# Expert results added to token rows in DRAM by accumulating DMAs, in place of a gather behind the last tile

## What is computed

```python
xn = rms_norm(x, norm2_g)
# router: one of 4 groups, then the top 2 of its 4 experts; combine[token, expert] is the weight, zero elsewhere
y = 0
for e in range(16):
    h = silu(xn @ w_gate[e]) * (xn @ w_up[e])        # 1024 -> 512
    y = y + combine[:, e:e+1] * (h @ w_down[e])      # 512 -> 1024
x = x + y
out = rms_norm(x, final_norm_g)
```

## Time and profile before

| | us |
|---|---|
| median of 3 runs (791.05 to 791.95) | 791.48 |
| the profiled execution, its own time | 791.86 |
| its span in the profile | 789.3 |
| PE busy | 764.9 (97%) |
| DVE busy | 493.4 (63%) |
| ACT busy | 450.4 (57%) |
| POOL busy | 208.8 (26%) |

### The profile page before, as it was taken

How to read it: one execution, slowest core, us unless ns; L and a number is a source line. 1 busy time by engine, 2 the same in 40 slices (tenths; PEclk the granted TensorE clock), 3 DMA queues, 4 the chain that set the end, 5 groups by cost and what they waited for, 6 DMA issues and landing times.

```text
span 789.3 us, 10839 instructions
## 1 busy us (share of the span) xinstructions
PE 764.9 (97%) x3739; PEld 622.0 (79%) x3739; DVE 493.4 (63%) x702; ACT 450.4 (57%) x590; POOL 208.8 (26%) x124
## 2 busy tenths in 40 slices
PE   7999999999999999999999999999999999999994
PEld 4788777777787888888888788887778888888782
DVE  5704476576644302322022668999999999999888
ACT  5244656565553323323221546887888887888862
POOL 3644433232233444344442522000000000000033
PEclk9999999999999999999999999999999999999998
DMA  8569999782122253323327537999999999999965
GB/s 299 183 215 386 365 333 388 276 329 81 54 81 81 81 193 100 108 81 105 102 86 264 194 114 275 404 409 408 409 410 409 409 410 409 409 409 356 395 253 205
DMA packets 134318, 206.74 MB, mean 262 GB/s; under 512 B 10813, under 2 KB 65669, under 8 KB 134278
## 3 DMA queue, kind: packets, MB, share of 16 engines
q1 hardware_dynamic: 126084, 188.80, 65.7%
q10 hardware_dynamic: 5890, 9.04, 3.1%
q0 software_dynamic: 2304, 8.39, 2.9%
HBM read 157.95 MB, written 48.25 MB: 261 GB/s over the span
## 4 chain that ended last, share of the span: by engine, by line
PE 82%; DVE 7%; ACT 2%; ACTq 2%; issue 2%; DMA 2%; POOL 2%; DVEq 0%; SPq 0%; POOLq 0%
PE ps L1052 24%; PE ps L1054 24%; PE ps L1053 24%; DVE w_lo L389 3%; PE ps L1342 2%; PE ps L1146 1%; PE ps L1174 1%; PE ps L1157 1%; PE ps L1295 1%; POOL raw_mg L656 1%; PE ps L1269 1%; DMA x<-in_x 1%; PE ps L1349 1%; ACTq L877 1%; DVE xT_lo L1959 1%
## 5 line engine op out<-in xcount | busy, mean ns | idle before, releaser
L383 POOL TENSOR_TENSOR w_lo<-raw,w_hi 128x1024 fp32r<-128x1024 f32 x72 | 173.6, 2414 | 253.1 <-ACT w_hi L371 253.1
L371 ACT ACTIVATE w_hi<-raw 128x1024 fp32r<-128x1024 f32 x73 | 76.9, 1058 | 191.9 <-PE ps L1054 164.4
L1052 PE MATMUL ps<-xn_hi,w_hi 128*128 128x512 f32 x352 | 140.6, 399 | 0.0
L1054 PE MATMUL ps<-xn_hi,w_lo 128*128 128x512 f32 x352 | 137.2, 390 | 0.0
L1053 PE MATMUL ps<-xn_lo,w_hi 128*128 128x512 f32 x352 | 137.1, 389 | 0.0
L1052 PE MATMUL ps<-w_hi,xT_hi 128*128 128x512 f32 (+1 forms) x248 | 97.0, 391 | 2.2 <-DVE w_lo L389 2.2
L1054 PE MATMUL ps<-w_hi,xT_lo 128*128 128x512 f32 (+1 forms) x248 | 95.2, 384 | 0.0
L1053 PE MATMUL ps<-w_lo,xT_hi 128*128 128x512 f32 (+1 forms) x248 | 94.9, 383 | 0.0
L656 POOL DMA_INDIRECT raw_mg<-slots,slot_idx x7 | 7.8, 1117 | 280.4 <-DMA slots<-y_tile 278.6
L1052 PEld LDWEIGHTS ps<-xn_hi,w_hi 128*128 128x128 f32 x352 | 66.1, 188 | 16.2 <-issue 2.0
L1053 PEld LDWEIGHTS ps<-xn_lo,w_hi 128*128 128x128 f32 x352 | 66.1, 188 | 14.0 <-issue 1.0
(11 more groups left out here) (311 smaller groups left out, 1476.3 us busy)
## 6 DMA issues: line engine op xcount, KB each, us to landing
slots<-raw SPq DMA_DIRECT2D x65, 512.0 KB, 7.2
raw<-in_w_in SPq DMA_DIRECT2D x52, 512.0 KB, 4.1
raw_mg<-in_exp_w_down SPq DMA_DIRECT2D x35, 512.0 KB, 11.0
raw<-in_exp_w_gate SPq DMA_DIRECT2D x29, 512.0 KB, 11.6
raw_a<-in_exp_w_gate SPq DMA_DIRECT2D x26, 512.0 KB, 11.0
raw_c<-in_exp_w_up SPq DMA_DIRECT2D x24, 512.0 KB, 11.9
raw_mg<-in_exp_w_up SPq DMA_DIRECT2D x22, 512.0 KB, 11.1
raw<-in_exp_w_up SPq DMA_DIRECT2D x15, 512.0 KB, 11.7
```

Source lines behind the costliest of these rows:

```text
L371: nc.scalar.activation(w_hi[:, b % HI_SLOTS, :], raw_buf(b), ACT.Copy)\
L383: eng.tensor_tensor(w_lo[:, b % HI_SLOTS, :], raw_buf(b), w_hi[:, b % HI_SLOTS, :].bitcast(F32), ALU.subtract)\
L1052: pe.matmul(dst, hi_l, hi_r, start=start, stop=False)
L1054: return pe.matmul(dst, lo_l, hi_r, start=False, stop=stop)
```

## The change

**Weights with the slots.** A DRAM tensor `info` holds, for each slot, the token's number and its weight (8 bytes). POOL fills it with "no token" (numbers from 512 up, weight 0) during the mixer, scatters the 1024 real entries with 8 indirect DMAs behind `weighed`, reads the whole back into `slot_info` (64 KB) and raises `info_in`. For this the weights are worked out before tile 1 and no longer between tiles 4 to 6. ACT waits for `info_in` ahead of the first block that it splits inside `tile(at_odd(0), 0)`.

**Adding in DRAM.** SP stores `x_rows` (the residual) to a DRAM tensor `acc` in two halves of 1 MB. Behind each tile ACT's copy out of PSUM multiplies by the row's weight (same instruction, with `scale`), into one buffer `y_home`, and POOL adds the 128 rows to their tokens' rows in `acc` by one indirect DMA with `compute_op=add`, one after the other. ACT no longer stores.

**The end.** When the tile before the last has been added, SP loads all of `acc` into `x_rows`, and these rows are normed and written out. POOL gathers from `acc` the rows of the last tile's own 128 tokens (`z_home`); the last tile's result is added to them by DVE, they are normed apart, and written by an indirect DMA over the rows just written. The selection matrix, its matmuls and the gathers from `slots` go.

The core of the diff:

```diff
@@ SP
+            sp.dma_start(acc[TOK:TOK + P, :], raw[:, 4, :]).then_inc(S["zeros_stored"], 16)
+            def store_x2(half):
+                at = slice(512 * half, 512 * (half + 1))
+                sp.wait_ge(S["x2_done"], NT * (half + 1))
+                sp.dma_start(acc[0:TOK, at].rearrange("(t p) n -> p t n", p=P), x_rows[:, :, at])\
+                  .then_inc(S["acc_in"], 16)
             for r in range(8):
                 if r == RAW_MIX + 1:
+                    store_x2(0)
                     sp.wait_ge(S["w_used"], B_EXP)
                 load_block(ODD, r, tile_source(1, 0, r))
+            store_x2(1)
...
+            sp.wait_ge(S["y_added"], n_stop * 16 + 16 * (PAIRED - 1))
+            for t in range(NT):
+                sp.dma_start(x_rows[:, t, :], acc[t * P:(t + 1) * P, :]).then_inc(rows_in[t], 16)
@@ POOL
+            pool.wait_ge(S["info_filled"], 16)
+            pool.wait_ge(S["weighed"], 2)
             for t in range(NT):
-                gather(0, y_lo(t), t)
-                gather(1, y_hi(t), t)
+                for k in range(2):
+                    pool.indirect_dma_start(
+                        info, bass.IndirectOffsetOnAxis(ap=info_idx[:, 0, 2 * t + k:2 * t + k + 1], axis=0),
+                        pick_info[:, t, k, :], None).then_inc(S["info_out"], 16)
+            pool.wait_ge(S["info_out"], 16 * 2 * NT)
+            pool.dma_start(info_words, info.rearrange("(p b) n -> p (b n)", p=P)).then_inc(S["info_in"], 16)
+            def add_result(j, block):
+                if j is not first:
+                    pool.wait_ge(S["y_added"], j * 16)
+                pool.tensor_copy(tokens[:, :], info_words[:, bass.ds(block * 2, 1)]).then_inc(S["tokens_in"], 1)
+                pool.wait_ge(S["acc_in"], 32)
+                pool.wait_ge(S["tokens_in"], j + 1)
+                pool.wait_ge(S["y_act"], j + 1)
+                pool.indirect_dma_start(acc, bass.IndirectOffsetOnAxis(ap=tokens[:, 0:1], axis=0), y_home, None,
+                                        compute_op=ALU.add).then_inc(S["y_added"], 16)
...
+            pool.wait_ge(rows_in[0], 32)
+            link(pool.tensor_tensor(y_weighed, x_rows[:, 0, :], gf_rows[:, :], ALU.mult))
+            y_power(0)
+            pool.wait_ge(S["y_rstd"], 1)
+            pool.tensor_scalar(y_weighed, y_weighed, stat[:, 7, 0:1], None, ALU.mult).then_inc(S["y_norm_pool"], 1)
+            for t in range(1, NT):
+                y_power(t)
+            pool.wait_ge(S["z_stat"], 1)
+            pool.tensor_tensor(stat[:, 4, 3:4], stat[:, 4, 2:3], minus_half[:, :], ALU.pow).then_inc(S["z_rstd"], 1)
+            pool.wait_ge(S["z_norm"], 2)
+            pool.wait_ge(S["y_out"], 16 * NT)
+            pool.indirect_dma_start(out[0], bass.IndirectOffsetOnAxis(ap=last_info[:, 0:1], axis=0), z_weighed, None,
+                                    bounds_check=TOK - 1, oob_is_err=False).then_inc(S["z_out"], 16)
@@ ACT, y_part
-                act.wait_ge(at.y_free, at.y_count)
-                act.activation(at.y, ps[:, 5:7, :].rearrange("p a n -> p (a n)"), ACT.Copy).then_inc(S["y_act"], 1)
-                act.wait_ge(S["y_act"], n + 1)
-                act.dma_start(slots[bass.ds(block * P, P), :], at.y).then_inc(at.y_free, 16)
+                act.wait_ge(S["tokens_in"], n)
+                act.activation(y_home, ps[:, 5:7, :].rearrange("p a n -> p (a n)"), ACT.Copy,
+                               scale=info_words[:, bass.ds(block * 2 + 1, 1)].bitcast(F32)).then_inc(S["y_act"], 1)
             split_hi_loop(at_odd(0), AHEAD)
+            act.wait_ge(S["info_in"], 16)
             tile(at_odd(0), 0)
...
-            hT_hi_half(1)
-            for c in range(2):
-                act.wait_ge(S["w_used"], loop_block(tiles, 3 + c))
-                act.activation(xT_hi[:, 4 * c:4 * c + 4, :].rearrange("p k n -> p (k n)"), ps[:, 5 + c, :], ACT.Copy)\
-                   .then_inc(S["xT_hi_done"], 1)
+            y_square(0)
+            hT_hi_half(1)
+            for t in range(1, NT):
+                y_square(t)
@@ DVE
             overflow_count()
-            overflow_tiles(0, block_table, NE * PER_EXPERT)
+            info_rows()
+            share_of(0)
+            share_of(1)
+            combine_weights()
             for r in range(AHEAD):
                 split_lo_loop(at_odd(0), r)
...
+            y_normed(1)
+            y_normed(2)
+            dve.wait_ge(S["z_in"], 16)
+            z_sum(0)
+            z_weigh(0)
+            y_normed(3)
+            z_sum(1)
+            z_weigh(1)
```

More of the change, by code:

```diff
@@ L294, in build @@
             "x_even_in x_odd_in xT_ps xT_hi_done xT_done silu_done hid_done hT_ps hT_hi_done hT_done "
-            "y_act y_even_stored y_odd_stored y_last_stored before_last_stored sel_ps sel_done z_ps "
-            "y_sum y_sq y_stat y_rstd y_norm y_out dve_chain").split()}
+            "acc_in info_filled weighed info_out info_in tokens_in y_act y_added z_in "
+            "y_sq y_rstd y_norm_pool y_norm_dve z_sum z_weighed z_sq z_stat z_rstd z_norm y_out z_out pool_chain dve_chain").split()}
         raw_in = [sem(f"raw_in{s}") for s in range(RAW_MIX)]
@@ new lines, in block_of @@
+            def block_of(i):
+                return pool.value_load(block_table[0:1, bass.ds(i + 1, 1)], min_val=0, max_val=SLOT_TILES - 1)
+            first = 0
+            add_result(first, 0)
+            add_result(1, PER_EXPERT)
+            pool.wait_ge(S["tab"], 1)
+            n_stop = pool.value_load(tile_table[0:1, 0:1], min_val=NE - PAIRED, max_val=MAX_TILES - PAIRED)
+            with pool.Fori(2, n_stop + (PAIRED - 1)) as j:
+                add_result(j, block_of(j))
+            last_block = block_of(n_stop + (PAIRED - 1))
@@ L1850, in full_tables @@
                 dve.tensor_copy(tile_table[:, 1:NE + 1], row(23, NE)).then_inc(S["tab"], 1)
-            def last_tile():
-                for n in range(2):
-                    dve.tensor_scalar(last_rows[:, n:n + 1], four(2)[:, 0:1], 0.0,
-                                      float((NE - 1) * PER_EXPERT), ALU.is_equal, ALU.mult)
-                link(dve.tensor_tensor(weight, over, row(25, NE, PER_EXPERT - 1), ALU.mult))
-                link(dve.tensor_reduce(last_rows[:, 2:3], weight.rearrange(flat), AX.X, ALU.max))
@@ L1859, in last_tile_rows @@
-            def last_tile_rows():
-                for n in range(2):
-                    link(dve.tensor_tensor(last_rows[:, n:n + 1], last_rows[:, n:n + 1], last_rows[:, 2:3], ALU.max))
-                    dve.tensor_scalar(last_rows[:, n:n + 1], last_rows[:, n:n + 1], float(P), float(n * P),
-                                      ALU.mult, ALU.add)
-            at_first, at_second = top_slot[:, :, 1], top_slot[:, :, 0]
-            swap, apart = four(6), four(7)
-            in_last, place_last, stored = four(11), four(12), four(13)
@@ L1892, in choose_last, with info_rows @@
-            def choose_last():
-                for t in range(NT):
-                    last = dve.tensor_scalar(one_hot[:, t * P:(t + 1) * P], count_row[:, :], place_last[:, t:t + 1],
-                                             None, ALU.is_equal)
-                last.then_inc(S["routed"], 1)
+            def info_rows():
+                at = info_idx[:, 0, :]
+                dve.tensor_scalar(at, slot_idx[:, :], P - 1, 6, ALU.bitwise_and, ALU.logical_shift_left)
+                link(dve.tensor_scalar(info_idx[:, 1, :], slot_idx[:, :], 7, None, ALU.logical_shift_right))
+                link(dve.tensor_tensor(at, at, info_idx[:, 1, :], ALU.bitwise_or))
@@ L1919, in combine_weights @@
                 for k in range(2):
-                    link(dve.tensor_tensor(w_first[:, k, :], w_first[:, k, :], total, ALU.mult))
+                    dve.tensor_tensor(pick_info[:, :, k, 1].bitcast(F32), w_first[:, k, :], total, ALU.mult)\
+                       .then_inc(S["weighed"], 1)
             x2_add(0, 0)
@@ new lines, in z_sum, with z_weigh @@
+            def z_sum(c):
+                at = slice(512 * c, 512 * (c + 1))
+                dve.wait_ge(S["w_used"], loop_block(tiles, 3 + c))
+                dve.scalar_tensor_tensor(out=z_home[:, at], in0=ps[:, 5 + c, :], scalar=last_info[:, 1:2].bitcast(F32),
+                                         in1=z_home[:, at], op0=ALU.mult, op1=ALU.add).then_inc(S["z_sum"], 1)
+            def z_weigh(c):
+                at = slice(512 * c, 512 * (c + 1))
+                dve.wait_ge(S["z_sum"], c + 1)
+                dve.tensor_tensor(z_weighed[:, at], z_home[:, at], gf_rows[:, at], ALU.mult)\
+                   .then_inc(S["z_weighed"], 1)
@@ new lines, in _ @@
+            y_normed(1)
[6 more added lines that the diff above has]
+            z_weigh(1)
+            dve.wait_ge(S["z_sq"], 2)
+            link(dve.tensor_tensor(stat[:, 4, 2:3], stat[:, 4, 0:1], stat[:, 4, 1:2], ALU.add))
+            dve.tensor_scalar(stat[:, 4, 2:3], stat[:, 4, 2:3], 1.0 / D, EPS, ALU.mult, ALU.add)\
```

(2 more changed lines are left out.)

234 lines of the change are left out of this document (75 added, 159 removed).

## The result

| | before | after |
|---|---|---|
| median of 4 runs, us | 791.26 (791.02 to 791.95) | 811.87 (810.71 to 813.61) |
| the profiled execution, us | 791.86 | 810.71 |
| its span, us | 789.3 | 808.7 |

The ratio is 1.0256 (95% interval 1.0232 to 1.0279): the change makes the kernel slower by some 20 us. The forecast was slower by 8.9 us. The time lies inside the wide range, 790 to 814, and outside the forecast's own, 793 to 808.

What follows compares the result with a forecast made beforehand. The tile loop goes at PE's pace, its loads leaving the DMA engines almost no room. Span 789.3 + 14.0 + 2.0 - 3.1 + 0 - 4.0 = 798.2, median forecast 800.4 us; own range 793 to 808, wide range 790 to 814.

Steps and rivals of the forecast that it cites:

- term 1: Entry of tile 1: ACT waits for the weights until 511.0, so PE begins 14.0 us later (bounds 7 and 23).
- term 6: Last tile and tail: POOL sets the pace and the span's end comes 4.0 us earlier (bounds -11 and +2).
- Term 2: After the idle time at tile 1, PE restarts at the 1.2 GHz level: 2.0 us, between 0 and 3.3.
- Term 3: DVE's small tables, which make PE wait between tiles, leave the loop except tile 1's: -3.1 us.
- Term 4: Adding DMAs in the loop: up to 15 transfers per tile, offset by the loads' lead, 0 us.
- 21 against 18: Tiles 2 to 13: 7 us to spare plus PE's 14 us standing, against 18 us of extra transfer time.
- Term 5: Router's stretch: two 1 MB residual stores and 7 more small POOL operations cost 0, or delay the scatter 1 us at most.
- upper bound of +2: Tail: if every small POOL operation takes 1.5 us, its effect is +2 us instead of -4.0.
- three signs of a wrong forecast: ACT's wait under 10 us, ACT waiting for loads in later tiles, or PE standing in the last tile for `hT_done`.
- Rival A: Loop: an adding transfer costs as much as three, DMA engines become the bound, another 12 to 13 us, 813; chance 0.15.
- Rival B: Entry of tile 1: 8-byte entries go out quickly, `info_in` at 502, PE 5 us late, 789.4; chance 0.12.
- Rival C: Last tile: the last add needs 10 us, ACT holds PE's last blocks, normed rows 4 to 5 us later, 805; chance 0.13.

Runs made afterwards that it cites:

- e9: The kernel before, with DVE's 45 small table operations issued one by one behind weight splits of tiles 1 to 5: 789.78 us, ratio 0.9972.
- e1: The changed kernel, with ACT waiting for the weights only ahead of the first result it weighs, at the end of tile 1: 806.93 us, ratio 1.018.
- e3: The changed kernel with its wait kept and the 15 indirect DMAs writing in place of adding (the sum left out): 806.32 us, ratio 1.0168.
- e5: The changed kernel with the second 1 MB residual store moved behind the first two loads of tile rows: 812.73 us, ratio 1.0256.
- e4: The changed kernel with the first square of the normed rows behind the second half of the hidden values on ACT: 810.24 us, ratio 1.0216.
- e10: The kernel before, with each of the 14 results ACT stores in the loop stored a second time, no add: 805.67 us, ratio 1.0153.

## Why the prediction was wrong in size

The direction was right, and so was the forecast's main mechanism, the wait for the weights at the entry of tile 1. The forecast span was 798.2, the measured one 808.7: 10.5 us are missing. Two terms hold nearly all of it: 4.5 in term 1, of which 2.4 are landings, and 5.5 in term 6.

| term | forecast | measured | miss |
|---|---|---|---|
| 1. wait for the weights | +14.0 | +18.5 | +4.5 |
| 2. slow restart | +2.0 | +1.6 | -0.4 |
| 3. tables leave the loop | -3.1 | -3.3 | -0.2 |
| 4. adds in the loop | 0 | +1.0 | +1.0 |
| 5. router's stretch | 0 | 0 | 0 |
| 6. last tile and tail | -4.0 | +1.5 | +5.5 |

(The measured column is the ledger's; its first line is parted into terms 1 and 2, its last two make term 6.)

- **Term 1, mis-sized.** The way was right link by link: `weighed`, 8 scatters, landing, read back. `info_in` was forecast at 511.0 and came at 515.35. Of these 4.3 us, 0.8 lie between DVE's last row, at 493.4 as forecast, and POOL's first issue at 494.20, and 1.1 in the eight issues (one took 1.96 us). The other 2.4 are the two landings: "With 1 KB in all I take 3" was 4.6 behind the end of the last issue, and the read back, 4.3 with its issue in the forecast, took 5.1. I had the earlier trace rows with 6.0 us from a full loop and used it only as a bound. Beside these landings the core moves 405 to 408 GB/s. That the few bytes are slow because SP's loads keep the engines full fits this, but isn't shown: no run has the same transfers beside idle engines. The bounds of 7 and 23 us held.
- **Term 2** came out near: eight matmuls take 0.79 to 0.49 us, six of them 0.63, and cost 1.6 us. But the 2.0 was chosen between 0 and 3.3, so its closeness is in part luck. The row it came from the earlier trace rows doesn't show the lower level either: there the granted clock is on record as 1.00 from 10 to 15 us. **Term 3** was right to 0.2 us, and e9 shows its cause.
- **Term 4** was nearly right. The add costs two transfers, 15 per tile, and PE's standing still pays for it: "only because of term 1". e1 shows this from one side, e3 from the other. The step that failed is the lead, "21 against 18". PE stood longer than forecast, 15.8 us, but for the last 4.7 of them SP had no free buffer. An estimate from these rows: 7 + 15.8 - 4.7 = 18 us of lead against 12 times 1.55 (19.24 less 17.69), 18.6. So it ran out in tiles 13 and 14, and 1 us was missed.
- **Term 5** came out at 0 for another reason than given, by luck. The store does collide: PE's first rows come 1.8 us late. But the wait of term 1 is longer and swallows it (e5).
- **Term 6, wrong in size and sign.** Four steps failed.
  - The copy: "leave 10 us to spare" holds in the loop and not in the last tile, where ACT is ready for its next copy 9.3 us behind the one before. It stands 1.94 us for that one's add, and the copy comes 0.6 us late; with plain writes it comes 1.15 us earlier (e3).
  - The add: "with the landing of a gather, 5.4, it is in at 762.5" has 6.6 us from the copy to the landing. It took 8.5 (1.9 to the issue's start, 6.6 from there).
  - POOL's operations: from the first rows' landing to the third power I had 8.6 us, and it took 10.1. The scaling "taken at 1.8" was 2.86 us, and the first small operation of 128x1 took 1.04 us instead of 0.55.
  - The last scatter: from ACT's last scaling to the end I had 3.3 us, and it took 5.3 (0.85 to the issue's start at 804.28, 4.4 from there to the end of the span).

  The Trainium skill, SBUF — State Buffer (SBUF: two separate sides), which I had set beside the power's row, fits the small operation: it takes 0.19 us with DVE quiet and 1.28 us beside a DVE pass. The whole comes near the upper bound of +2 that I worked out in that place, but not by its condition, since the powers took 0.55 to 0.57 us; that is luck.
- **The signs named ahead.** Two of the three signs of a wrong forecast are there: ACT waits 2.7 us for loads in tiles 13 and 14, and PE stands in the last tile. The tail of 15 us behind the last matmul came out as forecast only because that matmul was itself 10 us later than forecast.
- **Rival A** (an add costs three): wrong in its price, since it is two. Its mechanism is real and is what remains as soon as the wait is repaired. **Rival B** fell: entries of 8 bytes take POOL 0.95 us or more each, so the time doesn't go with the bytes. **Rival C** did occur in its mechanism, though the add landed in 6.6 us and not in 10: PE stood 2.88 us in the last tile and ran its last blocks at 0.63 us. But e4 shows that this isn't what the end waits for.

Not tried: a shorter way for the weights than through DRAM, and adding with another kind of DMA. So what is left open is whether some form of this change could win. What the runs show is that every form tried that adds, and e10 with its 15 plain transfers per tile, has a median of 804 us or more.

## What to carry to other kernels

An accumulating DMA cost the DMA engines two transfers here, so count it twice before you put one into a loop whose loads already fill them. When a wait and a load on the DMA engines come with one change, each can hide the other: remove the wait in the forecast and price again what is left. Price a small transfer that must land before work goes on by a row from an equally loaded stretch, not by the quickest row of its kind. And when a buffer is single, look for the place where its two uses stand closest, not at the average tile.

## What the runs showed of the hardware

- An indirect add of 512 KB: 13.1% of the engines' time in 40 us for two of them, against 6.4% for two plain stores and 12.8% for four. Two plain indirect writes of the same rows take 6.4% too (e3). The add's issue takes POOL 1.57 us (median) against 0.96 for the plain write. Its landing takes 8.9 us (median) in the loop, 6.6 at the least, the plain one's 6.8 and 3.3.
- A scatter of 128 entries of 8 bytes lands in 5.1 to 6.2 us where the core moves some 380 to 408 GB/s, and a read of 64 KB in 5.1 us.
- Behind a stop of PE of 15.8 us the granted clock is 0.50, and the work runs at this level for 3 us, which costs 1.6 us.
- POOL's operation on 128x1 numbers takes 0.19, 1.04 or 1.28 us within 10 us of each other, by what runs beside it.
